# Weights loaded with the contraction index split as half, partition and row of four, in two DMAs per slot

## What is computed

```python
def layer(x, mod, l, ...):
    shift1, scale1, gate1, shift2, scale2, gate2 = jnp.split(mod, 6, axis=-1)
    u = x * (1 + scale1) + shift1
    m, ... = _mixer(u, w_in[l], ..., w_branch[l], w_out[l], ...)
    x = _layernorm(ALPHA * x + gate1 * m, ln_g[l, 0], ln_b[l, 0])
    h = x * (1 + scale2) + shift2
    f = _moe(h, router_w, router_b, w_gate[l], w_up[l], w_down[l])
    return _layernorm(ALPHA * x + gate2 * f, ln_g[l, 1], ln_b[l, 1])

# mod = silu(c) @ w_mod[l] + b_mod[l], for the two groups of tokens
# the experts, as the reference writes them (gates is zero but for two experts of a token):
act = silu(einsum('nd,edf->nef', tok, w_gate)) * einsum('nd,edf->nef', tok, w_up)
out = einsum('nef,efd->nd', act * gates[..., None], w_down)
```

## Time and profile before

| | us |
|---|---|
| median of 3 runs (lowest, highest) | 2439.3 (2438.86, 2439.33) |
| span of the profiled execution | 2440.0 |
| TensorE matmul busy | 2189.8 (90%) |
| VectorE, ScalarE, POOL busy | 806.6, 448.7, 214.7 |
| moved by DMA | 407.08 MB, 401.72 MB of it read from HBM |
| packets | 197,474, of which 210 have 8 KB or more |

### The profile page before, as it was taken

One profiled execution on the slowest core, in us unless ns is written; L12 is line 12 of the kernel. 1 busy time (PEld: TensorE's weight loads), 2 busy tenths in 40 slices (PEclk: granted clock), 3 DMA queues, 4 the chain that ended last, 5 costly groups with the idle time before them and its releaser, 6 DMA issues.

```text
span 2440.0 us, 25315 instructions
## 1 busy us (share of the span) xinstructions
PE 2189.8 (90%) x9696; PEld 1211.5 (50%) x9696; DVE 806.6 (33%) x1602; ACT 448.7 (18%) x857; POOL 214.7 (9%) x221
## 2 busy tenths in 40 slices
PE   4998899998999879999699889999899978999994
PEld 1557774544444444344355777454444454344342
DVE  0526651625011421111552665162501250111115
ACT  0232114123100211011123111412300121111011
POOL 3024430000000000000002443000000000000000
PEclk9999999999999989999898999999999989999997
DMA  9321113144332359999722121313123228999993
GB/s 326 133 92 59 57 57 104 48 143 159 127 97 99 109 202 349 348 350 350 259 69 102 50 63 51 103 48 112 48 79 100 102 87 319 330 350 369 349 350 127
DMA packets 197474, 407.08 MB, mean 167 GB/s; under 512 B 6178, under 2 KB 6498, under 8 KB 197264
## 3 DMA queue, kind: packets, MB, share of 16 engines
q1 hardware_dynamic: 193136, 393.65, 45.9%
q0 software_dynamic: 4256, 12.28, 1.7%
HBM read 401.72 MB, written 4.19 MB: 166 GB/s over the span
## 4 chain that ended last, share of the span: by engine, by line
PE 72%; DMA 11%; DVE 10%; ACT 3%; issue 2%; SPq 1%; POOL 1%; DVEq 0%; POOLq 0%; ACTq 0%
PE bank L395 24%; DMA ring<-in_exp_w_up 10%; PE bank L545 6%; PE bank L885 6%; PE bank L913 6%; PE bank L873 5%; PE bank L497 5%; PE bank L805 5%; PE bank L923 2%; PE bank L431 1%; PE bank L581 1%; DMA ring<-in_w_mod 1%; PE bank L702 1%; PE bank L712 1%; PE bank L758 1%
## 5 line engine op out<-in xcount | busy, mean ns | idle before, releaser
L395 PE MATMUL bank<-ring,xt 128*128 128x512 f32 x1440 | 623.3, 593 | 8.5 <-ACT shared L1328 2.8
L395 PEld LDWEIGHTS bank<-ring,xt 128*128 128x128 f32 x1440 | 272.2, 190 | 354.2 <-issue 351.8
L885 PE MATMUL bank<-ring,shared 128*64 128x512 f32 x1280 | 295.5, 605 | 54.1 <-DMA ring<-in_exp_w_gate 29.9
L885 PEld LDWEIGHTS bank<-ring,shared 128*64 128x64 f32 x1280 | 88.1, 138 | 254.9 <-issue 167.6
L545 PE MATMUL bank<-shared 128*128 128x128 f32 x1408 | 184.2, 287 | 13.5 <-DVE shared L1678 5.5
L545 PEld LDWEIGHTS bank<-shared 128*128 128x128 f32 x1408 | 176.2, 201 | 15.8 <-issue 15.6
L1929 DVE TENSOR_TENSOR shared<-shared,bank 128x512 f32<-128x512 f32 x20 | 13.8, 688 | 444.6 <-PE bank L885 444.6
L913 PE MATMUL bank<-ring,shared 128*64 128x512 f32 x640 | 141.7, 595 | 1.2 <-issue 1.2
L873 PEld LDWEIGHTS bank<-qkvp,shared 128*128 128x128 f32 x1056 | 124.6, 198 | 20.2 <-issue 17.9
L873 PE MATMUL bank<-qkvp,shared 128*128 128x128 f32 x1056 | 128.8, 284 | 3.8 <-DVE qkvp L1916 3.8
L497 PE MATMUL bank<-xt,ring 128*128 128x384 f32 x384 | 124.3, 486 | 2.8 <-DVE xt L1525 2.8
(11 more groups left out here) (342 smaller groups left out, 2119.1 us busy)
## 6 DMA issues: line engine op xcount, KB each, us to landing
ring<-in_exp_w_gate SPq DMA_DIRECT2D x80, 1024.0 KB, 7.9
ring<-in_exp_w_up SPq DMA_DIRECT2D x80, 1024.0 KB, 9.8
ring<-in_exp_w_down SPq DMA_DIRECT2D x80, 1024.0 KB, 10.7
ring<-in_w_in SPq DMA_DIRECT2D x32, 2048.0 KB, 9.5
ring<-in_w_mod SPq DMA_DIRECT2D x24, 2048.0 KB, 8.0
ring<-in_w_branch SPq DMA_DIRECT2D x6, 2048.0 KB, 7.7
ring<-in_w_out SPq DMA_DIRECT2D x4, 2048.0 KB, 7.7
shared<-in_ln_g POOLq DMA_DIRECT2D x4, 512.0 KB, 3.8
```

Of the source, the lines that this page charges most:

```text
L395: mm = pe.matmul(ps[:, 0:width], xtv[:, k, t * P:(t + 1) * P], w_of(k), start=(k == 0), stop=(k == KC - 1))
L885: mm = pe.matmul(ps[u * SLOTS:(u + 1) * SLOTS, :], xg[:, at:at + SLOTS], w[:, u, k, :], start=(part == k == 0), stop=(part == 1 and k == 3))
```

## The change

Four things are done, in one edit.

1. **The contraction index** of `w_in`, the router, the expert gate and up weights is split as half*512 + partition*4 + row (`in_rows`), that of the expert down weights as partition*4 + row. In an expert load a partition's four rows now lie together: one run of 8 KB in place of four of 2 KB. A `w_in` load takes 512 of 8240 columns, so its runs stay 2 KB; `w_mod`, `w_out` and `w_branch` keep their split and their runs.
2. **The tokens follow.** `transpose_x` and `turned` read every fourth column as a transpose's operand, `mod_columns` does for the modulation's shift and scale (not for the two gates), and the bias is turned with eight transposes of 24 rows in place of one of 96, with five copies in place of one behind it.
3. **The down weights** are cut by rows in place of columns, so `output` makes both halves of the result from each chunk, and the two banks are summed side by side. A new semaphore `expert_down_used` tells SP when the first of the two chunks has been used.
4. **Each dense load** is issued as two DMAs of 1 MB; a slot's semaphore counts 32 per filling. The POOL queue's narrow `w_in` loads and the router's are two DMAs each, too.

```diff
+        xq = x[:, :].rearrange("p (t a q b) -> p t a q b", t=T, a=2, q=P)
...
-            first = 16 * (n // RING + 1)
-            eng.wait_ge(slot_in[n % RING], first if e is None else e * 32 + first)
+            eng.wait_ge(slot_in[n % RING], 32 * (n // RING + 1))
...
-                        mm = pe.transpose(ps[:, t * P:(t + 1) * P], xv[:, t, k * P:(k + 1) * P], c("ident"))
+                        mm = pe.transpose(ps[:, t * P:(t + 1) * P], xq[:, t, k // 4, :, k % 4], c("ident"))
...
-                    mm = pe.matmul(mod_bank[:, at:at + 2], mrow[:, b * P:(b + 1) * P], c("fold", 0, 2), start=True, stop=True)
+                    cols = mrow[:, b * P:(b + 1) * P] if j // 2 in (2, 5) else mrow[:, :].rearrange("p (q b) -> p q b", b=4)[:, :, b]
+                    mm = pe.matmul(mod_bank[:, at:at + 2], cols, c("fold", 0, 2), start=True, stop=True)
...
-                        mm = pe.transpose(ps[:, m * P:(m + 1) * P], hact[:, m * P:(m + 1) * P], c("ident"))
+                        mm = pe.transpose(ps[:, m * P:(m + 1) * P], hact.rearrange("p (q m) -> p q m", m=4)[:, :, m], c("ident"))
...
-                    for half in range(2):
-                        w = chunk(q, 4 + half)
-                        for m in range(4):
-                            for u in range(2):
-                                at = m * P + u * SLOTS
-                                mm = pe.matmul(banks[EXPERT_BANKS["out"][half]][u * SLOTS:(u + 1) * SLOTS, :], ht[:, at:at + SLOTS],
-                                               w[:, u, m, :], start=(m == 0), stop=(m == 3))
-                        mm.then_inc(sem("expert_out_full"), 1)
+                    for part in range(2):
+                        w = chunk(q, 4 + part).rearrange("p u (m x) n -> p u m (x n)", m=2)
+                        for i in range(2):
+                            m = part * 2 + i
+                            for half in range(2):
+                                for u in range(2):
+                                    at = m * P + u * SLOTS
+                                    mm = pe.matmul(banks[EXPERT_BANKS["out"][half]][u * SLOTS:(u + 1) * SLOTS, :], ht[:, at:at + SLOTS],
+                                                   w[:, u, i, half * W5:(half + 1) * W5], start=(m == 0), stop=(m == 3))
+                                if m == 3:
+                                    mm.then_inc(sem("expert_out_full"), 1)
+                        if part == 0:
+                            mm.then_inc(sem("expert_down_used"), 1)
...
+            in_rows = lambda w: w.rearrange("(a p b) n -> p a b n", a=2, b=4)
...
-                sp.dma_start((ring_dn if name == "branch" else ring_in)[slot], source[name](l, j)).then_inc(slot_in[slot], 16)
+                to, of = (ring_dn if name == "branch" else ring_in)[slot], source[name](l, j)
+                n = to.shape[1] // 2
+                for part in range(2):
+                    cut = slice(part * n, (part + 1) * n)
+                    sp.dma_start(to[:, cut, :], of[:, cut, :] if name in ("mod", "out", "branch") else of[:, part, :, :])\
+                        .then_inc(slot_in[slot], 16)
...
-                        src = rows(a["exp_w_gate" if j < 2 else "exp_w_up"][l, e])[:, part * 4:(part + 1) * 4, :]
+                        src = in_rows(a["exp_w_gate" if j < 2 else "exp_w_up"][l, e])[:, part]
                     else:
-                        src = rows(a["exp_w_down"][l, e])[:, :, part * W5:(part + 1) * W5]
+                        src = a["exp_w_down"][l, e].rearrange("(p m) n -> p m n", m=4)[:, part * 2:(part + 1) * 2, :]
...
-                elif j in (1, 2):
-                    sp.wait_ge(sem("expert_out_full"), q * 2 + j)
+                elif j == 1:
+                    sp.wait_ge(sem("expert_down_used"), q + 1)
+                elif j == 2:
+                    sp.wait_ge(sem("expert_out_full"), q * 2 + 2)
```

More of the change, by code:

```diff
@@ L477, in _ @@
             pe.wait_ge(sem("mod_bias_in"), 16)
-            pe.transpose(ps[:, 0:96], otok[0:96, 0:P], c("ident")[0:96, 0:96]).then_inc(ready, 1)
+            for b in range(4):
+                pe.transpose(ps[:, b * 24:(b + 1) * 24], otok[0:24, 0:W5].rearrange("p (q b) -> p q b", b=4)[:, :, b], c("ident")[0:24, 0:24])
+            for b in range(4):
+                mm = pe.transpose(ps[:, 96 + b * 24:120 + b * 24], otok[0:24, b * P:(b + 1) * P], c("ident")[0:24, 0:24])
+            mm.then_inc(ready, 1)
             for l in range(DEPTH):
@@ L485, in _ @@
                     pe.wait_ge(sem("consts_in"), 16)
-                pe.wait_ge(sem(f"params{l}_in"), 16 * 7)
+                pe.wait_ge(sem(f"params{l}_in"), 16 * 9)
                 ps, ready = take(pe, ("taps", l))
@@ L974, in _ @@
             sp.dma_start(crow[8:16, :], a["c"].rearrange("b (k p) -> (b k) p", p=P)).then_inc(sem("cond_in"), 16)
-            sp.dma_start(otok[0:96, 0:P], a["b_mod"].rearrange("l (j p) -> (l j) p", p=P)).then_inc(sem("mod_bias_in"), 16)
+            sp.dma_start(otok[0:24, 0:W5], a["b_mod"].rearrange("l (j p) -> (l j) p", p=W5)).then_inc(sem("mod_bias_in"), 16)
             rows = lambda w: w.rearrange("(k p) n -> p k n", p=P)
+            in_rows = lambda w: w.rearrange("(a p b) n -> p a b n", a=2, b=4)
             source = {
                 "mod": lambda l, j: rows(a["w_mod"][l])[:, :, j * W5:(j + 1) * W5],
-                "qkv": lambda l, j: rows(a["w_in"][l])[:, :, j * W5:(j + 1) * W5],
-                "merge": lambda l, j: rows(a["w_in"][l])[:, :, IN_COL["merge"] + j * W5:IN_COL["merge"] + (j + 1) * W5],
+                "qkv": lambda l, j: in_rows(a["w_in"][l])[:, :, :, j * W5:(j + 1) * W5],
+                "merge": lambda l, j: in_rows(a["w_in"][l])[:, :, :, IN_COL["merge"] + j * W5:IN_COL["merge"] + (j + 1) * W5],
                 "out": lambda l, j: rows(a["w_out"][l])[:, :, j * W5:(j + 1) * W5],
@@ L985, in _ @@
             for name in ("gqk", "gv", "z", "r", "dq", "dk", "dv"):
-                source[name] = lambda l, j, name=name: rows(a["w_in"][l])[:, :, IN_COL[name]:IN_COL[name] + W5]
+                source[name] = lambda l, j, name=name: in_rows(a["w_in"][l])[:, :, :, IN_COL[name]:IN_COL[name] + W5]
             def load(key):
@@ L1064, in _ @@
                 pin = sem(f"params{l}_in")
-                pool.dma_start(smv[:, l, :, 0:16], a["w_in"][l, :, IN_COL["ba"]:IN_COL["ba"] + 16].rearrange("(k p) n -> p k n", p=P)).then_inc(pin, 16)
-                pool.dma_start(smv[:, l, :, 16:48], a["w_in"][l, :, IN_COL["lr"]:IN_COL["lr"] + 32].rearrange("(k p) n -> p k n", p=P)).then_inc(pin, 16)
+                for part in range(2):
+                    pool.dma_start(smv[:, l, part * 4:(part + 1) * 4, 0:16],
+                                   a["w_in"][l, part * W5:(part + 1) * W5, IN_COL["ba"]:IN_COL["ba"] + 16].rearrange("(p b) n -> p b n", b=4)).then_inc(pin, 16)
+                for part in range(2):
+                    pool.dma_start(smv[:, l, part * 4:(part + 1) * 4, 16:48],
+                                   a["w_in"][l, part * W5:(part + 1) * W5, IN_COL["lr"]:IN_COL["lr"] + 32].rearrange("(p b) n -> p b n", b=4)).then_inc(pin, 16)
                 pool.dma_start(convrow[:, l * P:(l + 1) * P], a["gdn_conv"][l].rearrange("k (c p) -> (k c) p", p=P)).then_inc(pin, 16)
@@ L1078, in _ @@
                     at += 128
-            pool.dma_start(rtv, a["router_w"].rearrange("(k p) e -> p k e", p=P)).then_inc(sem("router_in"), 16)
+            for part in range(2):
+                pool.dma_start(rtv[:, part * 4:(part + 1) * 4, :], a["router_w"][part * W5:(part + 1) * W5].rearrange("(p b) e -> p b e", b=4)).then_inc(sem("router_in"), 16)
             pool.dma_start(rbias[:, :], a["router_b"].partition_broadcast(P)).then_inc(sem("router_in"), 16)
@@ L1555, in _ @@
             ps, free = full(dve, "mod_bias")
-            dve.tensor_copy(bcol[:, :], ps[:, 0:96]).then_inc(free, 1)
+            link(dve.tensor_copy(bcol[:, :].rearrange("p (j b) -> p j b", b=4), ps[:, 0:96].rearrange("p (b j) -> p j b", b=4)))
+            own = ps[:, 96:192].rearrange("p (b l i a) -> p l i a b", b=4, l=DEPTH, i=6)
+            for l in range(DEPTH):
+                for i in (2, 5):
+                    ins = dve.tensor_copy(bcol[:, l * 48 + i * 8:l * 48 + i * 8 + 8].rearrange("p (a b) -> p a b", a=2), own[:, l, i])
+            ins.then_inc(free, 1)
             drained(dve, "mod_bias")
```

8 lines of the change are left out of this document (4 added, 4 removed).

## The result

The changed kernel takes 2411.8 us (median of 4 runs, 2404.8 to 2413.5) against 2439.3 us: a ratio of 0.9878, 95% interval 0.9861 to 0.9896. That is 27.6 us less. The profiled execution has a span of 2409.6 us.

What follows compares the result with a forecast made beforehand. TensorE, busy 90%, was taken as the bound, waiting for weights only at `w_mod` and in the expert stages. 2440.0 - 19.5 + 0.6 + 1 = 2422.1, less 0.7 for the median: 2421 us; own range 2414 to 2432, wide range 2410 to 2448.

Steps and rivals of the forecast that it cites:

- Where the gain lies: Only the two expert stages, 52.6 us of weight waits at most, could gain: -19.5 us; dense loads as two DMAs 0.
- Chunk 1: First gate-weight load of a turn, alone in the queue: lands 0.1 us sooner, bounds 0 and 0.39 us.
- larger gain: Rival: a lone load of 8 KB runs lands 0.4 us or more sooner; 2413 and down to 2400 us, chance 0.07.
- The packet: Full queue in the expert turns: 338 ns per 8 KB against 362 for four of 2 KB, 0.39 us less a chunk.
- The form of the sum: Each steady expert turn gains chunk 1's 0.1 us plus two queued chunks' 0.78, 0.88 us; 16 turns give 14.1 us.
- First turns: In two first turns up products of 5.35 and 5.30 us fall to 3.65: 2 x (0.88 + 1.7) = 5.2 us.
- Strided operands: Strided weight loads in `turned`, `transpose_x` and `mod_columns` stay hidden within a 0.11 us step: +1 us in all.
- the first rival: Each strided load in `turned`, `transpose_x` and `mod_columns` costs one more 0.11 us step: about 22 us, 2442, no change; chance 0.25.
- The sum: Whole kernel: 2440.0 - 19.5 (expert turns) + 0.6 (output by rows) + 1 (strided operands) = 2422.1, forecast 2421 us.

Runs made afterwards that it cites:

- the three pairs: Permuted writes into `mrow` and `hact` against the same kernel without: changed kernel 2404.1 to 2407.7 us, `back` moved early 2406.7 to 2412.3, `output` cut in two 2402.3 to 2412.6.
- the two traces: Two profiles of the unaltered changed kernel: its first measurement, 2411.8 us, and its rerun as base of the variants, 2407.7 us, ratio 0.9879 to the kernel before.

## Why the prediction was too small

*Where the gain lies: right.* It was put into the expert turns alone, and with the old index all of it is gone. No gain from a dense load was seen, and the split of them costs nothing (0.9998 by itself).

*Chunk 1: this step failed.* "For a lone load the nearest rows say that nearly nothing comes of it", and 0.1 us was taken. It became 1.0 us shorter. The step compared `w_branch` and `w_out`, single DMAs of 2 MB, 4 and 2 KB runs; both land after 7.7 us. Chunk 1 is two DMAs of 1 MB and took 8.36 us to its use, already slower than `w_out` with the same runs. That these rows did not fit could be seen from the earlier trace rows alone. As two DMAs of 1 MB the lone load takes 8.3, 7.5 and 7.3 us with 2, 4 and 8 KB (semaphore records).

The number of DMAs is not what sets chunk 1 apart: in the change `w_out` and `w_branch` are two DMAs of 1 MB, too, and come into an empty queue. The lines give the median of a 1 MB DMA from issue to landing, over both DMAs of a load, in this order: `w_out` (2 KB runs) and `w_branch` (4 KB) in the change, then chunk 1 of one turn with 2 KB (the kernel before), 4 KB and 8 KB (the change):

```profile
ring<-in_w_out SPq DMA_DIRECT2D x8, 1024.0 KB, 6.2
```

```profile
ring<-in_w_branch SPq DMA_DIRECT2D x12, 1024.0 KB, 6.0
```

```profile
ring<-in_exp_w_gate SPq DMA_DIRECT2D x2, 1024.0 KB, 6.5
```

```profile
ring<-in_exp_w_gate SPq DMA_DIRECT2D x2, 1024.0 KB, 6.0
```

```profile
ring<-in_exp_w_gate SPq DMA_DIRECT2D x2, 1024.0 KB, 5.8
```

With 4 KB the two kinds agree. With 2 KB all of `w_out` has landed after 7.7 us in the change (7.8 to 8.4 where the kernel before got the split), chunk 1 of a turn of the kernel before only after 8.1 to 8.6. So about half of the 1.0 us is something that gate weights in 2 KB runs have and `w_out` in as many DMAs, of the same size and runs, does not. What it is stays open; the reason that the prediction gave with "larger gain", fewer packets to start and to end, is not shown.

*The packet: right, a little small.* 338 ns were estimated, 320 measured, 381 GB/s became 422; 0.39 us a chunk in the queue was 0.45. The smaller price that a page of the Trainium skill gives ("DMA: Bandwidth & Descriptors", section "Why small descriptors are slow": 3 cycles a packet, an estimate of 0.2 us a chunk) is under half of that.

*The form of the sum: right, with the wrong first term.* A turn was to gain 0.1 + 2 x 0.39 = 0.88 us and gained 1.8. The three terms are those of the train in the table: 1.04 + 2 x 0.45. The rival "larger gain", a lone load that lands 0.4 us or more sooner, is what happened; it was given a chance of 0.07.

*First turns: right.* The up products of 5.35 and 5.30 us are gone; the up products in their place, both halves, take 7.26 us at 926.10 and 7.25 us at 2046.78. The prediction did not say what they were: behind the waits of 2.15 and 2.39 us the clock was at the lower of its two levels (granted 0.50 in 924 to 927 and in 2064 to 2067 us), and in the change it is 1.00 in 923 to 930.

*Strided operands: right for the transposes, wrong for `mod_columns`.* `turned` was to take 0.60 to 0.65 us and takes 0.64. For `mod_columns` the step "a load can grow by a third and stay hidden" was sound, but the load grew by 70%. There the first rival came true: one more step per load, 0.12 us on 128 loads. In all it cost some 4 to 10 us in place of 1, by the three pairs, of which one is clear. The rule named beside it, the Trainium skill's "Advanced Engine Details and Errata", section "Memory Cachelines" (two hits on a 16-byte line are needed), fits 329 ns at 16 bytes and 196 at 8. It does not fit the transposes, which are as slow at 8 bytes (194 ns) as at 16 (195).

*The sum.* 36.6 us of expert waits went, of which the prediction had 16.1 (its other 3.4 were the two slow products). By stage the experts are 41 and 43 us shorter in the two traces, and what came back stands ahead of layer 0's experts: 10.7 and 4.7 us. Part of it is the strided loads; the rest is open. The granted clock explains little of it: over the 66 runs of the kernel before the time falls by 0.7 us for each 0.001, and the means are 0.961 there and 0.959 over the eight runs of the changed kernel, by which I estimate 1 to 2 us. The two errors had opposite signs; the larger one won.

## What to carry to other kernels

When a ring of buffers is emptied and refilled in bursts, find the train: the loads from the first that is issued into an empty queue to the last that TensorE waits for. In this kernel its length plus the compute outside it was the turn, and a wait removed inside it only moved to the train's end. Price the train with rows of the very loads it is made of; rows of another tensor with as many DMAs of the same size and runs were 0.5 us off here. Check first that the rows you borrow reproduce its present length. A layout that lengthens runs can be paid for where data is written instead of where it is read as weights.

## What had not been expected of the hardware

A strided weight load costs differently by its kind. The loads of `mod_columns` take 192 ns packed, 196 with a step of 8 bytes, 329 with 16, those of the transposes, at their fastest, 137, 194 and 195. ScalarE's permuted copy of 128x512 took 597 ns, the same as the plain one. And a lone load of 2 MB in two DMAs gained more from 8 KB runs (1.0 us) than one in the full queue (0.45 us), and about half of that has another cause than the number of packets: `w_out` with as many landed some 0.5 us sooner.
